# FFN blocks: the T2 weight sum of four gate blocks on VectorE in place of a DMA, and two reorderings of splits

## What is computed

```python
D_FF_2 = 2816
def swiglu(h, w_gate, w_up, w_down):
    return (jax.nn.silu(h @ w_gate) * (h @ w_up)) @ w_down
x = x + 0.5 * swiglu(rmsnorm(x, norm_ffn1[layer]), ffn1_gate[layer], ffn1_up[layer], ffn1_down[layer])
```

## Time and profile before

| | us |
|---|---|
| runs shown, median | 3647.27 |
| profiled execution, its own time | 3649.27 |
| its span | 3647.4 |
| TensorE busy | 3543.2 |
| VectorE busy | 2513.1 |
| ScalarE busy | 1804.8 |
| the four FFN stretches | 1480 to 1840, 2225 to 2560, 2560 to 2900, 3290 to 3647 |

### The profile page before, as it was taken

One profiled execution on the slowest core, in us unless ns is written; L12 is line 12 of the kernel. 1 busy time (PEld: TensorE's weight loads), 2 busy tenths in 40 slices (PEclk: granted clock), 3 DMA queues, 4 the chain that ended last, 5 costly groups with the idle time before them and its releaser, 6 DMA issues.

```text
span 3647.4 us, 53611 instructions
## 1 busy us (share of the span) xinstructions
PE 3543.2 (97%) x20848; PEld 3028.1 (83%) x20848; DVE 2513.1 (69%) x3210; ACT 1804.8 (49%) x2527; POOL 285.7 (8%) x317
## 2 busy tenths in 40 slices
PE   9999899999999999999999999999999999999999
PEld 7776688888678887989977798999998977789988
DVE  4455666666755767787767577887888676578885
ACT  3335344436633444655555456555655554546554
POOL 0001000000200000100000220000000000310000
PEclk9999999999999999999999999999999999999999
DMA  4000256422005663577621016776777421017774
GB/s 185 36 35 35 92 162 183 140 105 93 24 35 173 173 174 117 172 199 221 176 87 57 12 53 172 201 217 179 204 204 194 133 106 50 2 63 210 207 197 132
DMA packets 70668, 475.18 MB, mean 130 GB/s; under 512 B 7952, under 2 KB 8336, under 8 KB 17552
## 3 DMA queue, kind: packets, MB, share of 16 engines
q1 hardware_dynamic: 46224, 303.97, 23.0%
q0 software_dynamic: 24192, 167.78, 21.0%
HBM read 404.62 MB, written 2.10 MB: 112 GB/s over the span
## 4 chain that ended last, share of the span: by engine, by line
PE 75%; DVE 16%; ACT 5%; DMA 2%; issue 2%; DVEq 0%; POOL 0%; ACTq 0%; SPq 0%; POOLq 0%
PE ps L670 73%; DVE split L2531 6%; ACT arena L1479 3%; DVE arena L2531 3%; PE ps L679 2%; DVE X L2535 2%; ACT split L1479 2%; DMA ring<-in_wts 2%; DVE arena L2535 2%; ACT L1479 1%; DVE arena L3629 0%; DVE ring L2531 0%; DVE small L2547 0%; DVE arena L2527 0%; DVE arena L2559 0%
## 5 line engine op out<-in xcount | busy, mean ns | idle before, releaser
L670 PE MATMUL ps<-split 128*128 128x512 f32 (+1 forms) x16236 | 2955.3, 341 | 51.2 <-DVE arena L2531 14.1
L670 PEld LDWEIGHTS ps<-split 128*128 128x128 f32 x16236 | 2506.9, 191 | 419.3 <-issue 60.3
L2531 DVE TENSOR_TENSOR split<-ring,split 128x1024 fp32r<-128x1024 f32 x674 | 823.0, 1221 | 422.7 <-ACT split L1479 372.6
L1479 ACT ACTIVATE split<-ring 128x1024 fp32r<-128x1024 f32 x674 | 709.7, 1053 | 720.9 <-PE ps L670 660.4
L1479 ACT ACTIVATE arena<-ps 128x512 f32<-128x512 f32 (+5 forms) x656 | 343.0, 523 | 377.1 <-PE ps L670 258.3
L670 PE MATMUL ps<-arena 128*128 128x128 f32 (+9 forms) x3344 | 485.5, 297 | 23.2 <-ACT arena L1479 8.8
L670 PEld LDWEIGHTS ps<-arena 128*128 128x128 f32 (+2 forms) x3344 | 393.8, 190 | 98.0 <-issue 65.6
L1479 ACT ACTIVATE split<-arena 128x1024 fp32r<-128x1024 f32 (+2 forms) x242 | 251.8, 1040 | 211.6 <-PE ps L670 131.4
L2531 DVE TENSOR_TENSOR split<-arena,split 128x1024 fp32r<-128x1024 f32 (+2 forms) x242 | 290.2, 1199 | 79.6 <-ACT split L1479 60.1
L2531 DVE TENSOR_TENSOR arena<-arena 128x512 f32<-128x512 f32 (+7 forms) x302 | 215.2, 713 | 32.7 <-ACT arena L1479 15.7
L2535 DVE SCALAR_TENSOR_TENSOR X<-ps,X 128x512 f32<-128x512 f32 x252 | 174.4, 692 | 69.0 <-PE ps L670 47.5
(11 more groups left out here) (114 smaller groups left out, 1214.2 us busy)
## 6 DMA issues: line engine op xcount, KB each, us to landing
ring<-in_wts SPq DMA_DIRECT2D x260, 1024.0 KB, 5.4
arena<-in_wts POOLq DMA_DIRECT2D x80, 1024.0 KB, 8.4
ring<-ring POOLq DMA_DIRECT2D x28, 1024.0 KB, 9.5
ring<-arena POOLq DMA_DIRECT2D x24, 1024.0 KB, 7.7
ring<-in_wts SPq DMA_DIRECT2D x41, 512.0 KB, 3.5
ring<-in_wts POOLq DMA_DIRECT2D x14, 1024.0 KB, 8.0
arena<-arena POOLq DMA_DIRECT2D x6, 1024.0 KB, 10.3
arena<-in_wts POOLq DMA_DIRECT2D x8, 512.0 KB, 4.5
```

The lines of the kernel that those rows point to most:

```text
L670: return e.matmul(out, l, r, start=start, stop=stop, skip_group_check=True)
L1479: o.sig(a.activation(out, i, f, **kw), sig)
L2531: o.sig(v.tensor_tensor(out, a, b, op), sig)
```

## The change

In gate blocks 1 to 4 of each FFN, T2 is now made by VectorE (`second`: b11's slot = T1 + b22, two additions of 128x1024): in round 2 of the blocks that a down block follows, in round 1 of the others. POOL makes no T2 transfer there, and its T4 waits for VectorE's `f_two` in place of `f_t2`. The slots of b12 and b22 come free only after `f_two`. The semaphore that the first block's accumulation used is renamed `f_open`. In the first block the low half of F5 goes ahead of the sum "sixth", and the steps of `whole` for F3 and F6 move back behind splits and behind ScalarE's copies of N5. In down blocks VectorE makes the split of N5's second half ahead of F6's.

```diff
@@ plan, ffn, block
             for pc in B.of[2]:
                 summed_up += 1
                 pc.sum = ("f_t1", summed_up)
+            B.adds = B.gated and w == 512 and not B.first
+            downs += 16 * (not B.adds)
+            for pc in next(of for (what, _, _), of in zip(B.order, B.of) if what == "P6"):
+                seconds += B.adds
+                pc.sum = ("f_two", seconds) if B.adds else ("f_t2", downs)
+            B.two = pc.sum
             for q, b, added in (("b11", "t2", "f_t4"), ("b12", "t1", None), ("b22", "b22", None), ("b21", "t4", None)):
                 B.loads[q].end, B.loads[q].added = ("lo", end[b]), added and (added, B.count)
+            if B.adds:
+                B.loads["b12"].added = B.loads["b22"].added = B.two
             return B
@@ scalar_program, ffn: first
             early(U, "P1", lambda t: F.part[:, 2 * t:2 * t + 2, :], 1.0)
-            next(extra)
             split(next(below))
             next(extra)
             split(next(below))
@@ scalar_program, ffn: gate_up
                 if wide and r == 5:
                     gated(U, 0, 0)
+                if U.first and r > 2:
+                    next(extra, None)
                 for y, _ in enumerate(() if U.first and r == 2 else U.of[r]):
                     split(next(below))
@@ vector_program
+    def second(U, q):
+
+        r = {b: K.RING[:, ld.slot, :] for b, ld in U.loads.items()}
+        v.wait_ge(S[f"ring{U.loads['b22'].slot}"], U.loads["b22"].landed)
+        p = U.of[2][q]
+        c = slice(p.q * U.w, (p.q + p.c) * U.w)
+        tt(r["b11"][:, c], r["b12"][:, c], r["b22"][:, c], ALU.add, "f_two")
@@ vector_program, ffn: whole
                 if g == 0:
+                    lo("f5", F.shape, 1)
                     tt(F.sixth, F.shape, F.a11, ALU.subtract, "h_sum")
-                    lo("f5", F.shape, 1)
+            yield
             tt(F.a12, F.sixth, F.a12, ALU.add, "h_sum")
             yield
             lo("f3", F.a12, 2)
@@ vector_program, ffn: first
             split(next(below))
             next(extra)
             split(next(below))
+            next(extra)
             split(next(below))
-            next(extra)
@@ vector_program, ffn: gate_up
                 if r == 2:
                     two(U)
+                if U.first and r > 2:
+                    next(extra, None)
...
                     if r + y == 0 and not U.before.gated:
                         next(late)
                         next(late)
+                    if U.adds and not U.first and r == (2 if D else 1):
+                        second(U, y)
                     if D and r == 4:
                         added_up(after, y)
@@ vector_program, ffn: down
             form(f5)
             split(next(below))
             read(U, "P1")
+            split(next(below))
             form(f6)
             split(next(below))
             tt(q["a12"], q["sum"], q["a12"], ALU.add, "shape")
-            split(next(below))
             split(next(below))
             form(f3)
@@ pool_program, block
         if U.first:
-            g.wait_ge(S["f_two"], begun)
+            g.wait_ge(S["f_open"], begun)
             g.dma_start(at["b11"], b22, accum_op=ALU.add).then_inc(S["f_t2"], 16)
...
+        g.wait_ge(*((S["used"], U.begin) if U.first else (S["lo"], U.before.split["t3"])))
+        g.dma_start(t3, b22).then_inc(S["f_base"], 16)
+        g.wait_ge(S["f_base"], U.count)
+        g.dma_start(t3, b12, accum_op=ALU.add).then_inc(S["f_t3"], 16)
+        if not U.adds and not U.first:
             g.wait_ge(S["lo"], U.split["b11"])
             g.wait_ge(S["f_t1"], U.of[2][-1].sum[1])
             g.wait_ge(S["f_t3"], U.count)
             g.dma_start(at["b11"], t3, accum_op=ALU.add).then_inc(S["f_t2"], 16)
         g.wait_ge(S["lo"], U.split["b21"])
-        g.wait_ge(S["f_t2"], U.count)
+        g.wait_ge(S[U.two[0]], U.two[1])
         g.dma_start(at["b21"], at["b11"], accum_op=ALU.add).then_inc(S["f_t4"], 16)
```

More of the change, by code:

```diff
@@ L245, in plan @@
     lins, loads, turned, forms, n = {}, [], [], [], 0
-    sums, shapes, before, blocks, summed_up, done, holds = 0, 0, None, 0, 0, 0, {}
+    sums, shapes, before, blocks, summed_up, seconds, downs, done, holds = 0, 0, None, 0, 0, 0, 0, 0, {}
     slots, held, kept = [0, 1, 2, 3], {}, {}
@@ L373, in ffn @@
     def ffn(l, n_):
-        nonlocal n, blocks, summed_up, shapes, done
+        nonlocal n, blocks, summed_up, seconds, downs, shapes, done
         key, new, us = f"fgu{n_}_{l}", [], []
@@ L405, in block @@
         def block(name, key, p, h, kbase, c1, c2, w, at=None):
-            nonlocal blocks, summed_up
+            nonlocal blocks, summed_up, seconds, downs
             blocks += 1
@@ L3893, in opened @@
         ld = U.loads["b11"]
-        g.dma_start(K.RING[:, ld.slot, 0:U.h * U.w], W["wts"][U.loads["b12"].i], accum_op=ALU.add).then_inc(S["f_two"], 16)
+        g.dma_start(K.RING[:, ld.slot, 0:U.h * U.w], W["wts"][U.loads["b12"].i], accum_op=ALU.add).then_inc(S["f_open"], 16)
     def block(U):
@@ L3901, in block @@
         if U.first:
-            g.wait_ge(S["f_two"], begun)
+            g.wait_ge(S["f_open"], begun)
             g.dma_start(at["b11"], b22, accum_op=ALU.add).then_inc(S["f_t2"], 16)
[L3904 to L3910, removed]
-            g.wait_ge(S["f_base"], U.count)
-            g.dma_start(t3, b12, accum_op=ALU.add).then_inc(S["f_t3"], 16)
+        g.wait_ge(*((S["used"], U.begin) if U.first else (S["lo"], U.before.split["t3"])))
[3 more added lines that the diff above has]
+        if not U.adds and not U.first:
             g.wait_ge(S["lo"], U.split["b11"])
@@ L4089 @@
            "ml_e", "ml_m", "ml_y", "ml_v", "ml_r", "ml_b", "ml_z", "power", "e_blk", "c_s", "c_e", "c_p", "n_m", "ln_x", "relu", "pt", "ple_x", "cq", "lat", "qrope", "qirope",
-           "ix_s", "ix_a", "isc", "gp", "madd", "a_m", "m_v", "od_a", "od_d", "xn", "again1", "again2", "t1", "t2", "t3", "t4", "fx_lo", "f_t1", "f_t2", "f_t3", "f_t4", "f_base", "f_two", "h_sum", "h_hi", "h_form", "early", "silu_u", "u", "shape", "fhi", "form", "part", "jn_a", "jn_d", "fx_s", "fx_m", "fx_r", "hc", "cv", "hi_v", "hp_a", "hp_d", "rw_a", "rw_d", "hv_a", "hv_d", "gp_a", "gp_d", "lr_a", "lr_d", "lru", "grow", "h67", "st", "kd", "hd", "he", "xl",
+           "ix_s", "ix_a", "isc", "gp", "madd", "a_m", "m_v", "od_a", "od_d", "xn", "again1", "again2", "t1", "t2", "t3", "t4", "fx_lo", "f_t1", "f_t2", "f_t3", "f_t4", "f_base", "f_open", "f_two", "h_sum", "h_hi", "h_form", "early", "silu_u", "u", "shape", "fhi", "form", "part", "jn_a", "jn_d", "fx_s", "fx_m", "fx_r", "hc", "cv", "hi_v", "hp_a", "hp_d", "rw_a", "rw_d", "hv_a", "hv_d", "gp_a", "gp_d", "lr_a", "lr_d", "lru", "grow", "h67", "st", "kd", "hd", "he", "xl",
            "oh", "sq", "bbr", "s0x", "s1", "kw", "xi", "xd", "gz", "gn_a", "gn_d", "ct", "state", "og_t", "og", "done", "out"]
```

## The result

The changed kernel takes 3711.92 us (median of 5 runs, 3704.36 to 3714.54), the kernel before 3650.47 in as many runs beside it: ratio 1.0168, 95% interval 1.0153 to 1.0183. Forecast were 3685 us and a range of 3658 to 3704. The direction held; the size was missed by 27 us, and the time lies 8 us above the range.

The account below looks back on a forecast made before the run. TensorE bounds the kernel, busy for 97% of the span, with 34 us of pauses in the FFNs as the most to win. Terms 42.1 - 4.2 = +37.9 us on the 3647.3 us median gave 3685.2 us, range 3658 to 3704.

Parts of the forecast that it names:

- The term of +42.1 us: T2 on VectorE in blocks 1 and 3: eight pauses of 6.6 us, 52.8 us in place of 10.7.
- Landing: Down block's b12, loaded together with b11 and beside T4, lands 12.0 us after f_two.
- Deadline: Blocks 1 and 3: b12 must land within 5.4 us of f_two, or TensorE pauses.
- the law: Blocks 1 and 3: where TensorE waits on the down block's b12, it resumes 8.85 us after that load lands.
- What stood there before: Pauses ahead of the last product of blocks 1 and 3 in the kernel before: 10.7 us in all.
- The term of -4.2 us: Down blocks, N5 split ahead of F6: all five pauses of 0.84 us in the third product go.
- First blocks, 0: First block of each FFN, reordered: no net effect, 0 us, within bounds of -8.5 and +1.6.
- Blocks 2 and 4, 0: T2 on VectorE in gate blocks 2 and 4: b11 issued up to 2.7 us later, nothing waits, 0 us.
- A: Rival, faster: down block's loads land in time and pauses go, -14.9 us, 3632 us; chance 0.07.
- C: Rival, hardly anything: T4 starts so late that the pair of loads is served first, +1 us, 3648 us; chance 0.05.
- B: Rival, slower by less: accumulation hurts no more than a load, landing 9.9 us, +21 us, 3668 us; chance 0.15.
- D: Rival: VectorE becomes the bound as well, late P6 splits, pauses of 9 us or more, from 3704 us up; chance 0.06.

Follow-up runs that it names:

- e1: The changed kernel without its three reorderings, so T2 on VectorE alone: 3708.82 us, ratio 1.0161 to the kernel before.
- e3: e1 with T2 back on the DMA in blocks 1 and 3, so on VectorE only in blocks 2 and 4: 3645.24 us, ratio 0.9987.
- e4: e1 with POOL's T4 of blocks 1 and 3 held until the down block's b12 has landed: 3692.35 us, ratio 1.0118.
- e5: e1 with the two T2 additions of blocks 1 and 3 made one round earlier, in round 1: 3655.71 us, ratio 1.0020.
- e2: The kernel before with the three reorderings alone, T2 by DMA as before: 3652.26 us, ratio 1.0005.
- e10: The kernel before with the change's down-block order and the read of N5 put behind the next split: 3648.80 us, ratio 0.9996.
- e7: The changed kernel with the down block's sum b11+b12 moved from round 4 to the end of round 6: 3695.49 us, ratio 1.0126.
- e8: e5 with the down block's sum b11+b12 moved from round 4 to the end of round 6: 3671.35 us, ratio 1.0061.
- e6: The kernel before with the down block's sum b11+b12 moved from round 4 to the end of round 6: 3659.74 us, ratio 1.0028.

## Why the prediction was right or wrong

**The mechanism: right.** Each place it named is there: two pauses in P7 and ahead of N4 in all eight blocks, eight waits of VectorE (8.01 us in the block shown), b11 and b12 issued 0.42 us apart, 8 transfers where 24 were, 92 additions, no pause of 0.84. e1 shows that the T2 part alone makes the loss, e3 that only its blocks 1 and 3 do, e4 that T4 beside the loads makes b12 late (7.4 us after f_two without it, 13.1 with it), e5 that one round more of time takes the loss away.

**The size: two steps failed.** The landing of b12 was put at 12.0 us after f_two and measured 13.4, and the reordering of the down blocks was put at a gain of 4.2 us and cost 4.6. Of the 26.7 us between forecast and median the T2 term makes 8.4, the reordering 8.8, the first blocks 0.1; 6.2 lie between the comparison of spans and that of medians, and 3.2 in the median of the kernel before, 3650.47 instead of 3647.27.

**The term of +42.1 us was mis-sized: +50.5.** The working had 8 x (12.0 - 5.4) = 52.8 in place of 10.7. Measured:

- *Landing*, forecast 12.0 us after f_two: 12.98 + 0.42 = 13.40 on average. Eight times 1.4 is 11.2 us, the largest part of the miss. The estimate took each kind of transfer at its own full rate (5.0 + 4.9 us). The DMA view of the changed kernel for 1563 to 1575 us shows that they do not add up like this (queue: packets, MB, share of the 16 engines' time):

```profile
DMA packets 424, 3.15 MB, mean 262 GB/s; under 512 B 40, under 2 KB 40, under 8 KB 40
...
q1 hardware_dynamic: 288, 2.10, 56.6%
q0 software_dynamic: 136, 1.05, 42.0%
```

   The accumulation uses 0.42 x 12 = 5.0 us of the engines, as taken from the earlier trace rows. The two loads use 0.566 x 12 = 6.8 us for 2.1 MB, 309 GB/s, not the 420 of loads by themselves. The loads' 1.8 us more per block are about what was missing. Two more blocks give the same: 316 and 299 GB/s for the loads (1692 to 1705 and 2663 to 2676 us). The other estimate, 11.6 us, came from a block in which the loads did not start together.
- *Deadline*, forecast 5.4 us after f_two: 5.06. P7's second half was wanted at 1577.96 - 4.83 = 1573.13, N4 2.88 us later, and 8.85 us ahead of that is 1567.16; f_two stands at 1562.1. The issues came 1562.10 - 1560.82 = 1.3 us later on the clock, most of it because the block itself began later; against the deadline 0.34 remain. Eight times that is 2.7 us.
- *The pauses as such* were nearly right: 50.0 us against 52.8. The low clock behind them makes most of the difference: 24 products in 4.61 us where 2.9 is undisturbed, 1.7 us in the block shown and 16.6 in eight (57.0 in the table, less 40.4 of long pauses; 1.65 to 2.6 each). It falls in time in which TensorE would else have waited for N4: by the law N4 comes 8 x (13.40 - 5.06) = 66.7 us late with or without it, and the table has 69.5 in all.
- *What stood there before*, forecast 10.7: 19.0. The three pauses of 3.02 and 3.03 us were each followed by the low clock too, 2.6, 1.7 and 1.7 us; the rest are some 0.3 us in each of the other blocks, too short for a row of the timeline. Missed on both sides, it cancels in part: the new side was 16.7 too low, the old one 8.3, the term 8.4. The 34 us that the prediction allowed for any gain are not a strict bound for the same reason: time at the low clock counts as busy.

**The term of -4.2 us was wrong: +4.6.** The step that failed is the count of "all five go" as pure gain because "F6 moves back by 1.33 us and is wanted a product later". The five did go. But VectorE had no gap behind them, so the same lag came out ahead of N3, eight times 0.90 to 1.27 us. e2 shows this without T2, and e10 that one more exchange passes it on again. The prediction looked at the one instruction in front of the pause and not at the next idle time of VectorE, and in the block shown there is none before N3's splits: the next, of 0.42 us, ends at 1623.39.

**First blocks, 0: right in the number** (+0.1), and in part by luck. N3 waits for the landing in both orders; ScalarE and TensorE of FFN 2, layer 0, in the changed kernel, answering to the earlier trace rows:

```profile
2250.93 6.01 PE L678 MATMUL ps<-split 128*128 128x256 f32 x48 [0.79 <-DVE split L2540]
...
2254.58 1.06 ACT L1487 ACTIVATE split<-ring 128x1024 fp32r<-128x1024 f32 x1 [2.55 <-DMA ring<-in_wts]
...
2258.05 1.29 ACT L1487 ACTIVATE arena<-ps 128x512 f32<-128x512 f32 x2
...
2258.79 3.46 PE L678 MATMUL ps<-split 128*128 128x256 f32 x27 [1.86 <-ACT arena L1487]
```

From the split behind the landing to the copies 3.47 us (3.48 in the earlier trace rows), and the pauses are 0.79 and 1.86 where they were 0.96 and 1.91. The 0.2 saved ahead of N5 is the forecast 0.3 at most. But three of the four first blocks of the changed kernel now pause for 0.41 to 0.55 us ahead of P6, the delay that the prediction had only as its upper bound. Three first blocks took 0.2 to 0.5 us more than before. The block above took 1.1 us less all the same, because behind the 1.91 us of the kernel before the clock was low (0.69 in the window 2245.95 to 2251.40) and behind the 1.86 it was not (1.00 in 2258.79 to 2264.20). **Blocks 2 and 4, 0: right** (e3).

**The rest of the miss.** 50.5 + 4.6 + 0.1 = 55.2 us is the difference of the spans. The medians differ by 61.4. The profiled execution has the lowest time of its kernel; the other four, at mean clocks of 0.988 to 0.989 against its 0.992, took 7 to 10 us more. Whether the many low-clock stretches have to do with that was not tried; e4 with 0.987, e1 with 0.989 and e7 with 0.990 have long pauses too, the kernels without them 0.993 to 0.996. One profile speaks against it: e1's, at 0.989 and a span of 3708.3, needs 2407.8 us outside the FFNs and so no more inside them than the changed kernel; its excess lies where no code differs, and e5, without a long pause, needs 2409.3 there. The cause of these 6.2 us stays open.

**The rivals.** A and C fell with the landing. B (an accumulation costs like a load) fell: no landing was under 12.7 us after f_two. D came nearest in its number and not in its cause: no late P6 split shows in any of blocks 1 and 3. The Trainium skill's rule, weighed in the prediction ("DMA: Bandwidth & Descriptors", Anatomy of one DMA), gives 9.2 us for the three transfers; the trace has 13.4. On another page ("Collectives: The Full Stack", "The bandwidth ceiling") the Trainium skill says that a reduce-scatter runs at half the rate of an all-gather because its add needs two source reads; the 208 to 213 GB/s against 420 here agree with that, though these are accumulations on one core and no run tries the cause.

## What to carry to other kernels

Moving a small transfer onto an idle engine also moves the moment at which its operands' buffers come free. Read which loads start from that moment, what else starts then, and which instruction stands in an engine's queue until they land; here one round earlier was worth 53 of the 59 us that e1 lost. Size several transfers that start together by their shares in a stretch where they do overlap, not by their separate rates, and give each consumer its own deadline: holding T4 back won 16 us and left another consumer late.

And when a reordering removes a pause, look for the next idle time of the engine that was late. If there is none before the next product that needs it, the pause moves and does not go.

## Hardware behaviour that was not expected

**A pause of TensorE of 3 us cost up to 2.6 us more, and its length alone doesn't decide it.** Behind each idle time of 2.99 us and above in the FFNs of these traces the granted clock was low; in the windows above it is 0.50 to 0.70, and in the kernels before and after the cost was 1.65 to 2.6 us for each. Shorter ones went both ways. Windows of e8 (behind a pause of 2.38 us), e6 (behind one of 2.38 as well) and e10 (behind one of 2.93):

```profile
1594.64:1600.00 5.36, 5.36 (x17) 4.24 (x18) 4.94 (x5) 3.83 (x4) 0.86 (x1) 0.68 0.60 122
```

```profile
1596.07:1599.00 2.93, 2.93 (x13) 2.46 (x14) 2.72 (x3) 1.63 (x2) 0.00 (x0) 1.00 0.88 179
```

```profile
3501.29:3506.80 5.51, 5.51 (x45) 5.47 (x46) 5.01 (x5) 4.25 (x5) 0.30 (x1) 1.00 0.85 149
```

The same edit made eight pauses of 2.18 to 2.38 us in e6, and four of them were followed by the low clock (P2 took 1.6 us longer there) and four were not. What decides is not shown. The Trainium skill ("TensorE: Matmul & The Clock Gate", The HAM clock gate) says that the array falls to 1.2 GHz when idle; the trace agrees for the long pauses, and for the shorter ones only in part.

**Loads slow down beside an accumulation beyond their share of time**: 299 to 316 against 420 GB/s for the engine time they use, in three blocks, while the accumulation keeps its 208 to 213.
